# Where the halves of a split activation lie: adjacent high and low parts, at two places modulo 256 bytes

## The reference, cut to what matters

```python
def swiglu_ffn(x, w_gu, w_down):
    gate, up = jnp.split(x @ w_gu, 2, axis=-1)
    return (jax.nn.silu(gate) * up) @ w_down

x = layer_norm_2(DEEPNORM_ALPHA * x + y, ...)                      # y: the mixer's output
x = layer_norm_2(DEEPNORM_ALPHA * x + swiglu_ffn(x, ...), ...)
```

## Time and profile before

| | |
|---|---|
| median of three runs | 864.12 us |
| the profiled execution | 864.27 us |
| its span, first to last instruction | 862.5 us |
| mean granted TensorE clock | 0.996 of full |
| TensorE matmul busy | 850.2 us, 99% |
| VectorE busy | 629.8 us, 73% |
| ScalarE busy | 426.5 us, 49% |
| DMA | 154.46 MB, 179 GB/s |

### The profile page before, as it was taken

One profiled execution on the slowest core, in us unless ns is written; L12 is line 12 of the kernel. 1 busy time (PEld: TensorE's weight loads), 2 busy tenths in 40 slices (PEclk: granted clock), 3 DMA queues, 4 the chain that ended last, 5 costly groups with the idle time before them and its releaser, 6 DMA issues.

```text
span 862.5 us, 13049 instructions
## 1 busy us (share of the span) xinstructions
PE 850.2 (99%) x5390; PEld 757.6 (88%) x5390; DVE 629.8 (73%) x880; ACT 426.5 (49%) x613; POOL 79.3 (9%) x81
## 2 busy tenths in 40 slices
PE   8999999999999999999999999999999999999996
PEld 7998999999988987878888988889988888889885
DVE  5999857688586675796777764678987777777445
ACT  6646454456664874435444453256553544445320
POOL 0340100122003001011000000031100200000000
PEclk9999999999999999999999999999999999999998
DMA  9963776664356752557556555386544765665531
GB/s 289 270 188 92 203 203 174 181 184 123 100 169 192 238 171 86 171 169 245 184 184 193 195 186 192 117 278 195 178 142 129 244 189 183 191 195 184 187 118 50
DMA packets 121989, 154.46 MB, mean 179 GB/s; under 512 B 11663, under 2 KB 98090, under 8 KB 121930
## 3 DMA queue, kind: packets, MB, share of 16 engines
q1 hardware_dynamic: 119978, 148.23, 56.4%
q0 software_dynamic: 1872, 5.26, 1.8%
q10 hardware_dynamic: 80, 0.13, 0.0%
HBM read 151.48 MB, written 1.05 MB: 177 GB/s over the span
## 4 chain that ended last, share of the span: by engine, by line
PE 94%; DVE 4%; DMA 1%; issue 0%; ACT 0%; SPq 0%; DVEq 0%
PE acc L597 19%; PE acc L599 19%; PE acc L598 19%; PE acc L635 15%; PE acc L639 8%; PE acc L720 1%; PE acc L717 1%; PE acc L718 1%; PE acc L668 1%; PE misc L798 1%; DMA x<-in_x 1%; DVE x L2191 1%; PE misc L857 1%; DVE y L2172 1%; DMA staged<-in_moba_w_in 1%
## 5 line engine op out<-in xcount | busy, mean ns | idle before, releaser
L1709 DVE TENSOR_TENSOR w_lo<-staged,w_hi 128x1024 fp32r<-128x1024 f32 (+1 forms) x274 | 331.6, 1232 | 134.6 <-ACT w_hi L1272 134.0
L1272 ACT CAST w_hi<-staged 128x1024 fp32r<-128x1024 f32 (+1 forms) x274 | 278.0, 1044 | 90.5 <-DMA staged<-in_ffn_w_down 44.2
L597 PE MATMUL acc<-x_parts,w_hi 128*128 128x256 f32 (+2 forms) x712 | 203.4, 286 | 0.0
L598 PE MATMUL acc<-x_parts,w_hi 128*128 128x256 f32 (+2 forms) x712 | 200.6, 282 | 0.0
L599 PE MATMUL acc<-x_parts,w_lo 128*128 128x256 f32 (+2 forms) x712 | 200.5, 282 | 0.0
L635 PE MATMUL acc<-x_parts,w_hi 128*128 128x512 f32 x576 | 196.3, 393 | 0.0
L639 PE MATMUL acc<-x_parts,w_lo 128*128 128x256 f32 x576 | 149.1, 279 | 0.0
L597 PEld LDWEIGHTS acc<-x_parts,w_hi 128*128 128x128 f32 x712 | 134.4, 189 | 1.7 <-issue 1.0
L598 PEld LDWEIGHTS acc<-x_parts,w_hi 128*128 128x128 f32 x712 | 134.0, 188 | 0.7 <-issue 0.2
L599 PEld LDWEIGHTS acc<-x_parts,w_lo 128*128 128x128 f32 x712 | 134.5, 189 | 0.0
L635 PEld LDWEIGHTS acc<-x_parts,w_hi 128*128 128x128 f32 x576 | 103.3, 188 | 18.4 <-DVE gate_sum L2352 0.2
(11 more groups left out here) (394 smaller groups left out, 1256.0 us busy)
## 6 DMA issues: line engine op xcount, KB each, us to landing
staged<-in_ffn_w_gu SPq DMA_DIRECT2D x88, 512.0 KB, 3.6
staged<-in_w_in SPq DMA_DIRECT2D x58, 512.0 KB, 3.8
staged<-in_ffn_w_down SPq DMA_DIRECT2D x44, 512.0 KB, 3.3
staged<-in_gla_w_in SPq DMA_DIRECT2D x24, 512.0 KB, 4.3
staged<-in_moba_w_in SPq DMA_DIRECT2D x24, 512.0 KB, 3.9
staged<-in_w_o SPq DMA_DIRECT2D x8, 512.0 KB, 3.9
staged<-in_gla_w_out SPq DMA_DIRECT2D x8, 512.0 KB, 3.8
staged<-in_moba_w_out SPq DMA_DIRECT2D x8, 512.0 KB, 3.8
```

The costliest lines, as they stand in the source:

```text
L597: pe.matmul(dst, st_hi, mv_hi, start=start, stop=False)
L598: pe.matmul(dst, st_hi, mv_lo, start=False, stop=False)
L1272: nc.scalar.copy(hi, raw).then_inc(rounded, 1)
L1709: nc.vector.tensor_tensor(lo, raw, hi, ALU.subtract).then_inc(split, 1)
```

## The change: what it does

The space of `x_parts` gets two more names for the time behind the first block: `ffn_split`, which starts at 0 modulo 256, and `mix_split`, 128 bytes further. Both are [8 chunks, 2 parts, 256 columns]: a chunk's high part and its low part lie side by side, 2,048 bytes per chunk, so every chunk and every part starts at the same place modulo 256. x2 and x4 (the inputs of the FFN) go to `ffn_split`, x1 and x3 (the inputs of the mixers) to `mix_split`. `with_both` now moves 512 adjacent columns. `x_parts` itself, as the first block uses it, moves from 192 to 0 modulo 256. No instruction, wait or transfer is added or removed. The ring's place is now asserted; it was there before, and so was `region`. Small constants are packed closer, and those between `x_parts` and `region` move by 64 to 192 bytes.

```diff
+        align(128)
         ring_at = cursor[0]
+        assert ring_at % 256 == 128
...
+        align(256)
+        parts_at = cursor[0]
         x_parts = place("x_parts", [2, KC, KEYS], F32R)
         x_hi, x_lo = x_parts[:, 0], x_parts[:, 1]
+
+        def split_at(past):
+
+            cursor[0] = parts_at + past
+            return place("x_split%d" % past, [KC, 2, ROWS], F32R)
+
+        ffn_split, mix_split = split_at(0), split_at(128)
+        cursor[0] = parts_at + 128 + 2 * KC * KEYS * 4
+
+        def split_of(tag):
+            return ffn_split if tag in ("x2", "x4") else mix_split
+
+        def high(tag):
+            return split_of(tag)[:, :, 0, :]
+
+        def low(tag):
+            return split_of(tag)[:, :, 1, :]
...
                         def with_both():
-                            return pe.matmul(acc[:, p, b, :].rearrange("p (s n) -> p s n", s=2), hi[:, c, cols],
-                                             x_parts[:, :, k, 0:ROWS], start=k == 0, stop=k == KC - 1)
+                            return pe.matmul(acc[:, p, b, :], hi[:, c, cols], ffn_split[:, k].rearrange("p s n -> p (s n)"),
+                                             start=k == 0, stop=k == KC - 1)
 
                         def with_high():
-                            return pe.matmul(acc[:, p, b, 0:ROWS], lo[:, c, cols], x_hi[:, k, 0:ROWS], start=False, stop=False)
+                            return pe.matmul(acc[:, p, b, 0:ROWS], lo[:, c, cols], ffn_split[:, k, 0, :], start=False, stop=False)
...
-            xt_hi, xt_lo = x_hi[:, :, 0:ROWS], x_lo[:, :, 0:ROWS]
+            xt_hi, xt_lo = high("x1"), low("x1")
...
-                t_stage(FIRST[tag] + COUNT[tag] - 4, 4, OUT["gate%d_%d" % (layer, LAST_H)], xt_hi, xt_lo)
+                rows = "x2" if layer == 0 else "x4"
+                t_stage(FIRST[tag] + COUNT[tag] - 4, 4, OUT["gate%d_%d" % (layer, LAST_H)], high(rows), low(rows))
```

More of the change, by code:

```diff
@@ L194, in hybrid_stack, with align @@
     with ExitStack() as ctx:
-        cursor = [(nc.sbuf_base + 63) // 64 * 64]
+        cursor = [nc.sbuf_base]
+        def align(to):
+            cursor[0] = (cursor[0] + to - 1) // to * to
         def place(name, cols, dt=F32):
             cols = [cols] if isinstance(cols, int) else list(cols)
+            size = int(np.prod(cols)) * 4
+            align(64 if size >= 256 else 32)
             t = nc.alloc_sbuf_tensor_at(name, [P] + cols, dt, offset=cursor[0])
-            cursor[0] += (int(np.prod(cols)) * 4 + 63) // 64 * 64
+            cursor[0] += size
             return t
+        align(128)
         ring_at = cursor[0]
+        assert ring_at % 256 == 128
         staged = place("staged", [RING, SLOT])
@@ L213, in hybrid_stack @@
         y = place("y", [TILES, DM])
+        align(256)
+        parts_at = cursor[0]
         x_parts = place("x_parts", [2, KC, KEYS], F32R)
         x_hi, x_lo = x_parts[:, 0], x_parts[:, 1]
+        def split_at(past):
[9 more added lines that the diff above has]
+            return split_of(tag)[:, :, 1, :]
+        align(64)
         norm_at = cursor[0]
@@ L716, in n_first @@
                                     if part == 0:
-                                        pe.matmul(dst, xt_hi[:, k, rows], w_hi[:, sl.ring(), cols], start=k == 0, stop=False)
-                                        pe.matmul(dst, xt_hi[:, k, rows], w_lo[:, sl.ring(), cols], start=False, stop=False)
+                                        pe.matmul(dst, high(tag)[:, k, rows], w_hi[:, sl.ring(), cols], start=k == 0, stop=False)
+                                        pe.matmul(dst, high(tag)[:, k, rows], w_lo[:, sl.ring(), cols], start=False, stop=False)
                                     else:
-                                        mm = pe.matmul(dst, xt_lo[:, k, rows], w_hi[:, sl.ring(), cols], start=False,
+                                        mm = pe.matmul(dst, low(tag)[:, k, rows], w_hi[:, sl.ring(), cols], start=False,
                                                        stop=k == KC - 1)
@@ L1477, in round_rows @@
                 await_full(act, name)
-                nc.scalar.copy(x_hi[:, lo:lo + n, t * P:t * P + P], bank(name)[:, 0:n * P]
+                nc.scalar.copy(high(tag)[:, lo:lo + n, t * P:t * P + P], bank(name)[:, 0:n * P]
                                .rearrange("p (c r) -> p c r", c=n)).then_inc(s["x_rounded"], 1)
@@ L2115, in rest_rows @@
                 dve.wait_ge(s["x_rounded"], 5 * (int(tag[1]) - 1) + u + 1)
-                read(rest(x_lo[:, lo:lo + n, t * P:t * P + P], bank(name)[:, 0:n * P].rearrange("p (c r) -> p c r", c=n),
-                          x_hi[:, lo:lo + n, t * P:t * P + P]), name)
+                read(rest(low(tag)[:, lo:lo + n, t * P:t * P + P], bank(name)[:, 0:n * P].rearrange("p (c r) -> p c r", c=n),
+                          high(tag)[:, lo:lo + n, t * P:t * P + P]), name)
             dve.wait_ge(s["gain_scaled"], 1)
@@ L2515, in rest_tile0 @@
                     await_read(pool, "%s_%d" % (tag, j))
-                    nc.gpsimd.tensor_tensor(x_lo[:, 4 * j:4 * j + 4, 0:P], y[:, 0, j * 512:j * 512 + 512]
-                                            .rearrange("p (c r) -> p c r", c=4), x_hi[:, 4 * j:4 * j + 4, 0:P].bitcast(F32),
+                    nc.gpsimd.tensor_tensor(low(tag)[:, 4 * j:4 * j + 4, 0:P], y[:, 0, j * 512:j * 512 + 512]
+                                            .rearrange("p (c r) -> p c r", c=4), high(tag)[:, 4 * j:4 * j + 4, 0:P].bitcast(F32),
                                             ALU.subtract).then_inc(s["x_rest"], 1)
```

## The result

The changed kernel takes 865.83 us (median of 12 runs, 865.49 to 866.54) against 863.67 us for the kernel before (12 runs, 863.41 to 864.32). The ratio is 1.0023, 95% interval 1.0015 to 1.0031: it is **slower by 2.2 us**, where 860.8 us, 3.3 us faster, was forecast. The profiled execution has a span of 864.3 us, 1.8 us more than before.

The account below looks back on a forecast made before the run. TensorE's matmul pace was taken to bound the kernel; -2.9 (wide pairs), -1.0 (mixers, stationary) and +0.6 (mixers, moving) gave -3.3 us, so 860.8 us was predicted, with a range of 857.4 to 864.4.

Parts of the forecast that it names:

- What bounds the kernel: Whole kernel: TensorE, busy 99% of the span, sets the time by its matmuls' pace; no new wait follows.
- The wide pairs: FFN wide stages, 576 pairs of 512- and 256-column matmuls: 5 ns less each with chunks at 0, -2.9 us.
- the pairs lock into a bad step: Rival, wide stages: one place for all gives a repeated bad step, 7 ns a pair, 4.0 us; 867.7 us, chance 0.10.
- The rest of the change: In the slower rival's time, everything outside the wide pairs: 0.4 us won.
- Adjacency at nothing: Wide pairs: moving one run of 512 columns instead of two of 256 gains nothing.
- The rival that let it gain 6 ns a both: Wide pairs: the 512-column matmul falls to 381 ns without its break; -6.7 us in all, 857.4 us, chance 0.15.
- The moving use in the mixers: Mixers, some 600 matmuls moving 256 columns at 128: may cost 1.2 us, half taken, 0.6 us more.
- The stationary use in the mixers: Mixers, 288 matmuls with an activation chunk stationary at 128: 393 to 390 ns each, 1.0 us less.
- The FFN's first and last four slots: FFN, 96 matmuls with stationary chunks at 0 and 192 moving chunks at 0: no change taken for either.
- The first block: First block, where `x_parts` moves by 64 bytes: nothing, give or take 0.3 us.
- The writes: ScalarE, GpSimd and VectorE writes of the split activations at a 2,048-byte stride instead of 1,088: nothing.
- Lengths of records: TensorE matmuls: a difference in a record's length was taken to show a difference in pace, though ends are modelled.

Follow-up runs that it names:

- the first experiment: Against the changed kernel: x2, x3 adjacent at rotating places, x1 adjacent at 0, x4 at 0 with halves 8,192 bytes apart; 864.7 us, one run.

## Why the prediction was wrong, point by point

- **What bounds the kernel** held: TensorE's pace is the time, no new wait came up in the wide stages, and the stage differences (2.0 us) add up to the measured one (2.2, or 1.8 in the spans) within 0.2.
- **The wide pairs** are the step that failed: "if all chunks behave as those at 0 do now, a pair gets up to 7 ns shorter", -2.9 us. They got 2.3 ns longer, +1.3 us, by the starts nearly all of it behind the high matmuls. I had taken the 387 and 278 of single matmuls for properties of place 0. They were read where place 0 stands between 192 and 64. With one place throughout, 387 comes once in three inside a block, between 396 and 398, and the high records there are 281 to 285. The trace of before held the warning, behind a mean of 281 ns that I read as a constant: the inputs u all stand at 0, and the starts of the matmuls on `u_mla` were 115, 118, 122, 120 and 119 ns apart in turn (around 237 us), five steps from one place.
- **The rival "the pairs lock into a bad step"**, with a chance of 0.10, is the mechanism that came. Its place was right; its price, 7 ns a pair taken from the worst single records, was three times too large, which is why its 867.7 lay above the 865.8 measured. The rest of the change, put at 0.4 us won there, cost 0.7 and hid a part of that.
- **Adjacency at nothing** was right (101.19 and 101.91 us in the first experiment). The rival that let it gain 6 ns a both was wrong.
- **The moving use in the mixers**: half of 1.2 us was charged and 1.0 us came, near the upper end. **The stationary use in the mixers**: -1.0 forecast, -0.7 measured. **The FFN's first and last four slots**, put at nothing, cost 0.2 and 0.3 us, again because one place was read off a mixture.
- **The first block** at nothing was right, within 0.1 us. **The writes** at nothing were right too: ScalarE's casts into the split activation last 503 ns and GpSimd's subtractions 1,298 on average, against 503 and 1,295.
- **Lengths of records** overstate pace. The pair's sum of lengths rose by 4 ns, from 672 to 676, while its pace rose by 2.3; the ends are modelled. Starts are the surer measure.

## What to carry to other kernels

The cost of one instruction seen in a varied sequence can't be multiplied into a uniform one where its neighbours have a part in it: look first for stretches of the trace that are already uniform, and see whether their step is steady or a cycle. On such a kernel operand places are worth a sweep of a few short runs, two or more places in one kernel by stage, since the differences (100.97 to 102.38 us for the same stage) are far clearer in the stretches of one profile than in whole times. A good place alone is no guarantee: here the best single one (64, for the mixers) gave its good step only to some runs of matmuls, and for the wide stage every single place tried (0, 64, 96, 128, 192) was worse than the rotation that the kernel had from its chunk stride. That does not carry over from form to form: for the 256 columns of q and k, rotating takes 118.1 to 118.4 ns a step, and of the single places 0 and 128 take more (119.4 and 119.9), 160 less (116.8).

## What the runs showed of the hardware that was not expected

- 256-column fp32r matmuls at one place had steady steps of 113.3 ns (at 64) and 120 ns (at 128), and cycles at others: three steps at 0 (118, 120, 122 ns), five at 32 (116, 117, 119, 122, 120). The 512-column ones of the down product had 227, 227 and 226 ns, on average 226.7. The three steady steps are 17, 18 and 34 times 6.67 ns; whether something has that period was not tried, and it may be chance.
- At the same place and shape two steps, 113 and 118 ns, can each hold for many matmuls; which one holds changed where other matmuls came between.
- For the same sequence of matmuls, the distance between moving operand and weights set the pace, and not the place of either (101.92 and 102.23 us with the ring at either place; distances 128 and 0 are the ones tried this way). That places count modulo 256 fits the kernel before, where the chunks k = 5, 6 and 7 take 387, 392 and 396 ns a both as k = 1, 2 and 3 do, though their addresses differ from those by 256 bytes modulo 512. The distance is not all: at a distance of 128 the 256 columns of x1 (first experiment) have steps of 118, 120 and 122 ns, on average 120, and those on `u_mla`, whose weight blocks follow each other in another order, the five of the section before, on average 118.8. Why a distance gives a bad cycle stays open: loading half the weight columns took away only some 3.4 of 25.8 ns a pair.
